# Sample forgetting attention and sample memory attention run beside the two passes of the first projection

## What is computed

```python
# layer 0; h = rmsnorm(x); z = h @ fox_w_in  (q | k | v 1024 each, f 8, xq 512, gate 1536)
lf = log_sigmoid(f + b_f)
mix_p = fox_prompt(q, k, v, lf)                       # causal, decay by cumsum(lf)
k_past = cache_fox_k[page_table]; v_past = cache_fox_v[page_table]; lf_past = cache_fox_logf[page_table]
suf = flip(cumsum(flip(lf_past))) - lf_past           # sum of the gates behind each past key
s_past = q_s @ k_past * scale + suf + c_new           # samples: 8 heads x 4 queries x 2048 past keys
s_new = q_s @ k_new * scale + (c_new_q - c_new_k), causal
p = softmax(concat(s_past, s_new)); mix_s = p @ concat(v_past, v_new)
x = x + rmsnorm((concat(mix, mem_attend(xq, mk, mv)) * silu(gate)) @ w_out)
```

## Time and profile before

| | |
|---|---|
| median of 3 runs | 4196.71 us |
| the profiled execution | 4198.52 us |
| its span, first to last instruction | 4196.9 us |
| TensorE matmul busy | 3607.0 us (86%) |
| VectorE, ScalarE, POOL busy | 1889.5, 1344.0, 338.3 us |
| mean granted TensorE clock | 0.915 of full speed |
| p00 and p01 | 156 to 628 and 684 to 1245 us |
| prompt attention, sample attention | 1302 to 2084, 2084 to 2660 us |

### The profile page before, as it was taken

The page is one execution under the profiler, slowest core; times in us unless marked ns, Lnnn a source line. Parts: engine busy times, 40 slices in busy tenths (PEclk is TensorE's granted clock), DMA queues, the critical chain, the costliest instruction groups (busy, mean ns, idle before and its releaser), DMA issues. The chain is left out here.

```text
span 4196.9 us, 58583 instructions
## 1 busy us (share of the span) xinstructions
PE 3607.0 (86%) x19825; PEld 3129.9 (75%) x19825; DVE 1889.5 (45%) x3376; ACT 1344.0 (32%) x2451; POOL 338.3 (8%) x550
## 2 busy tenths in 40 slices
PE   5699996999986888888678888699599779996899
PEld 4699995888875777777667777488499768775687
DVE  3311114334214766666567878533311244574433
ACT  1211114433113555545345656211211243311111
POOL 0131000000000111101111111000000000131000
PEclk8799997999997999999888989699799889997899
DMA  4332224333323222222176777333222233475332
GB/s 141 98 90 88 92 81 139 123 96 113 121 71 98 82 82 97 107 87 95 32 280 238 269 246 258 112 110 113 73 92 94 94 123 113 144 225 159 125 106 77
DMA packets 385188, 523.10 MB, mean 125 GB/s; under 512 B 52799, under 2 KB 275008, under 8 KB 380423
## 3 DMA queue, kind: packets, MB, share of 16 engines
q1 hardware_dynamic: 317175, 398.59, 29.6%
q0 software_dynamic: 30624, 93.22, 6.4%
q10 hardware_dynamic: 37248, 29.37, 2.2%
HBM read 388.77 MB, written 132.68 MB: 124 GB/s over the span
## 5 line engine op out<-in xcount | busy, mean ns | idle before, releaser
L399 ACT ACTIVATE z_st_p<-bank 128x352 f32<-128x352 f32 (+1 forms) x320 | 165.5, 518 | 933.8 <-PE bank L372 933.5
L345 DVE CAST w_hi_p<-w_raw_p 128x1024 fp32r<-128x1024 f32 (+1 forms) x130 | 89.6, 689 | 772.9 <-PE bank L372 755.6
L1410 PE MATMUL bank<-w_hi_o,b_hi_o 128*128 128x512 f32 x816 | 328.3, 402 | 64.5 <-DVE w_lo_o L1452 64.4
L372 PE MATMUL bank<-h00hi,w_hi_p 128*128 128x352 f32 x984 | 318.2, 323 | 7.0 <-DVE w_lo_p L347 7.0
L1411 PE MATMUL bank<-w_hi_o,b_lo_o 128*128 128x512 f32 x816 | 324.2, 397 | 0.0
L1412 PE MATMUL bank<-w_lo_o,b_hi_o 128*128 128x512 f32 x816 | 324.0, 397 | 0.0
L372 PE MATMUL bank<-h00lo,w_hi_p 128*128 128x352 f32 x984 | 316.0, 321 | 0.0
L372 PE MATMUL bank<-h00hi,w_lo_p 128*128 128x352 f32 x984 | 315.7, 321 | 0.0
L372 PE MATMUL bank<-h01hi,w_hi_p 128*128 128x512 f32 x656 | 264.3, 403 | 9.2 <-DVE w_lo_p L347 7.9
L372 PE MATMUL bank<-h01hi,w_lo_p 128*128 128x512 f32 x656 | 256.3, 391 | 0.0
L372 PE MATMUL bank<-h01lo,w_hi_p 128*128 128x512 f32 x656 | 256.2, 391 | 0.0
(11 more groups left out here) (349 smaller groups left out, 8925.7 us busy)
## 6 DMA issues: line engine op xcount, KB each, us to landing
z<-z_st_p SPq DMA_DIRECT2D x128, 512.0 KB, 2.7
v_raw_sf<-in_cache_fox_v POOLq DMA_DIRECT2D x128, 512.0 KB, 4.9
k_raw_sf<-in_cache_fox_k SPq DMA_DIRECT2D x128, 512.0 KB, 5.0
w_raw_p<-in_fox_w_in SPq DMA_DIRECT2D x80, 512.0 KB, 4.0
b_raw_o<-bT SPq DMA_DIRECT2D x32, 768.0 KB, 7.4
w_raw_p<-in_pool_w_in SPq DMA_DIRECT2D x48, 512.0 KB, 4.7
out<-tok_fa ACTq DMA_DIRECT2D x64, 256.0 KB, 2.3
w_raw_o<-in_w_out ACTq DMA_DIRECT2D x24, 512.0 KB, 3.5
```

What stands on the lines that cost most here:

```text
L372: last = nc.tensor.matmul(out, wt[:, u, k, :], h[:, k, at0:at0 + width], start=(m == 0), stop=(m == MM - 1))
L399: nc.scalar.activation(z_st[:, t % 2, at0:at0 + width], src[:, 0:width], func).then_inc(z_read, 1)
L1410: nc.tensor.matmul(out, bh, w_hi[:, k, cols], start=(k == 0), stop=False)
```

## The change

Three things are moved. The samples' half of the gates, the suffix sums and the new keys and values become a work, `sample_gates`, in tiles 0 to 2 of p01. Sample attention becomes a work, `sample_fox`, in tiles 2 to 32 of p01: page s is transposed in step s, scored in the even step at or behind it with its neighbour, and the value page of step s is that of 19 steps before; it has one bank for scores instead of two, rings of 4 key and 3 value pages, and goes page by page over all samples without a loop. Memory attention of the samples goes from p01 to p00, tiles 18 to 39; that of the prompt to tiles 32 to 41 of p01. What stays of the gates, `prompt_gates`, is a block between p01 and prompt attention; it loads the forget rows from z, where the passes now store them. The comments in the diff are mine.

```diff
 def project_pass(..., stores, works=None, past_gates=None):        # forget=(bias_f, fT) is gone
-                width = FH if row is None else P
-                if row is not None:
-                    sp.wait_ge(z_read, C * (t + 1))
+                _, row, _, width = tiles[t]        # the forget tile is stored to z like any other, 8 rows
+                sp.wait_ge(z_read, C * (t + 1))
...
-def forget_gates(...)      # prompt and samples, a block of its own
+def prompt_gates(nc, const, banks, zT, f_row, bias_f, lf_prompt, cT):      # a block of its own
+            sp.dma_start(fT[:, :], zT[f_row:f_row + FH, 0:SEQ]).then_inc(f_in, 16)
...
-def sample_kv_out(...)     # a block of its own
+def sample_gates(...):     # a Work of 14 steps: sample gates, suffix sums, new keys and values
+            if i == STEPS - 1:
+                sp.wait_ge(row_d, 4)
+                for q in range(TN):
+                    sp.dma_start(sufT.rearrange("(r q) n -> q r n", q=TN)[q], suf_row[:, :]).then_inc(out_d, 16)
+                sp.wait_ge(out_d, 16 * (5 + TN))
...
-def sample_attention(...)  # a block of its own
+def sample_fox(...):       # a Work of STEPS = 3 + 128 + 22 = 153 steps
+    T_BANKS, S_BANK, O_BANKS, M_BANK = banks[0:2], banks[2], banks[3:5], banks[5]
+    def sp(sp):            # step i, s = i - 3
+            if i == 1:
+                for h in range(FH):        # 3 small loads per head: mask, c_key, c_qry
...
+            for x in (range(KR) if i == 0 else [s + KR - 1] if s >= 1 and s + KR - 1 < NPG else []):
+                sp.dma_start(k_raw[:, x % KR, :], cache_k[...]).then_inc(k_in[x % KR], 16)
+    def pe(pe):
+            if group(s) is not None:       # even s: scores of pages s - 2 and s - 1
+                pe.wait_ge(ktl_d, 2 * s)
+                for h in range(FH):
+                    nc.tensor.matmul(S_BANK[:, 0:2 * P], q, kT_hi[:, h, :], ...)
+                    nc.tensor.matmul(S_BANK[:, 0:2 * P], q, kT_lo[:, h, :], ...)
+            for b, p in products(s):       # value tile of page s - 19
+                pe.wait_ge(vl_d, y + 1)
+                for n in range(2):
+                    nc.tensor.matmul(O_BANKS[n][:, :], pr, v_hi[:, y % 2, vs], ...)
+                    nc.tensor.matmul(O_BANKS[n][:, :], pr, v_lo[:, y % 2, vs], ...)
+            if batch(s, 18) is not None:   # transposes of p into M_BANK
+                pe.wait_ge(pn_d, b + 1)
...
+            if 0 <= s < NPG:
+                if s:
+                    pe.wait_ge(ktl_d, 2 * s)
+                for n in range(2):         # 8 transposes of page s
+                        nc.tensor.transpose(T_BANKS[n][...], k_raw[:, s % KR, ...], ident[:, :])
+    def act(act):          # order in a step: kT_hi x2, low rows of the group, exp, pT, v_hi of step s + 1
+    def dve(dve):
+            if i == 2:
+                dve.wait_ge(kn_in, 16 * (1 + 3 * FH))
...
+            if 0 <= s < NPG:               # kT_lo, two halves, each behind its kT_hi
+                nc.vector.tensor_tensor(kT_lo[at], T_BANKS[n][...], kT_hi[at].bitcast(F32), ALU.subtract)
+            if group(s) is not None:
+                nc.vector.scalar_tensor_tensor(dst, dst, c_qry[:, b:b + 1], S_BANK[0:R, 0:2 * P], ALU.add, ALU.add)
+                nc.vector.tensor_tensor(dst, dst, low[0:R, :], ALU.add)
+                if g == NG - 1:            # new keys' scores, then the maximum over 2052 columns
+            if batch(s, 17) is not None:   # wait for exp, reciprocal, multiply 2052 columns
+            for b, p in products(s + 1):
+                dve.wait_ge(vh_d, y + 1)
+                nc.vector.tensor_tensor(v_lo[:, y % 2, :], v_raw[:, y % VR, :], v_hi[:, y % 2, :].bitcast(F32), ALU.subtract)
...
 # first pass (p00)
+                    sample, _ = sample_memory(0, ..., [(XQ + 2, 0), (len(tiles) - 2, 14)], lambda sp: landed(sp, XQ - 1))
 # second pass (p01)
-                        sample, ends = sample_memory(0, ..., [(0, 0), (8, 14)])
-                    prompt, _ = prompt_memory(0, ..., [(8, 0), (XQ + 1, 15), (30, 42)], ...)
+                        gates, ends_g = sample_gates(..., [(0, 0), (2, 14)])
+                        fox, ends_f = sample_fox(..., [(2, 0), (32, 153)], ends_g)
+                    prompt, _ = prompt_memory(0, ..., [(32, 0), (41, 42)], lambda sp: landed(sp, XQ - 1), ends_f)
-            forget_gates(...)
-        sample_kv_out(...)
+        prompt_gates(nc, const, banks, z0, F_ROW, fox_b_f, fox_lf_p, cT)
         fox_attention(nc, const, banks, z0, cT, bT, fox_k_p, fox_v_p)
-        sample_attention(...)
         output_projection(nc, "o0", ...)
```

## The result

The changed kernel takes 4256.8 us (median; 4249.6 to 4259.1) against 4196.8 (4194.2 to 4204.2): ratio 1.0137, 95% interval 1.0119 to 1.0155. Its profiled execution took 4249.6 us, its span is 4248.1: 51.2 more than the span before.

A forecast was written before the change was run, and what follows sets the result against it. In the second pass TensorE is busy 558 of 561 us, so added work costs at least its own TensorE time. -576.6 - 25 + 0 + 12 + 12 + 405 + 183 + 25 = +35: 4234 us, range 4105 to 4310.

The forecast's parts named there:

- The signs named beforehand: In the second pass, odd steps' value matmuls wait over 100 us for the value difference; pass takes 1110 to 1170 us.
- The old stage, -576.6, and the gates, -25: Removed between stages: the sample attention stage, 576.6 us, and 25 us of the 57.4 between second pass and prompt attention.
- Sample memory attention, 0: Moved from second pass to first, where it pays the same 40 us as before: zero in sum.
- Gates in tiles 0 to 2 and prompt memory attention, +12 each: Second pass: gates and new keys/values cost 12 us of TensorE (5 to 22); denser prompt memory attention +12 (0 to 25).
- The page steps, 405 + 183 + 25 = 613: Sample attention in the second pass: 405 us of TensorE's own time, 183 of waits, 25 of lost clock.
- Own TensorE work, 405: In sample attention 128 pages take TensorE 358 us and the further work per sample 47, together 405 us.
- Waits, 183: Waits in sample attention: 115 us between steps, 38 sample ends, 10 first steps and last sample, 20 start; bounds 0, 260.
- The clock, 25: Half rate after some waits of about 2.6 us or longer in sample attention costs 25 us, bounds 0 and 90.
- Cover of the weight splits, 0: In sample attention's steps the weight splits fit into VectorE's idle time and cost nothing; without that cover 57 us.
- Rival 1: Waits in page steps mostly hidden, VectorE's value tile being ready for the odd step: 4112 us, chance 0.27.
- Rival 2: The clock falls in most pairs of page steps, costing 90 us instead of 25: 4297 us, chance 0.13.
- Rival 3: Loads don't keep up at the start and sample ends of sample attention, costing 15 us: 4247 us, chance 0.05.

The follow-up runs named there:

- experiment 6: Kernel before the change, with sample memory attention alone moved from the second pass to tiles 18 to 39 of the first: 4202.4 us against 4199.4, ratio 1.0006.
- experiment 8: Changed kernel with the page steps of sample attention left out of the pass, result columns filled with gate rows: 3620.5 us.
- 1, values first: Changed kernel with ScalarE's copy and VectorE's difference of the next value tile ahead of the work on the key transposes: 4115.2 us, ratio 0.9807.
- 2, longer in even steps: Changed kernel with the difference of the value tile computed twice at the end of even steps 20 to 126: 4347.0 us.
- 7, denser: Changed kernel with the 153 steps of sample attention in 24 tiles instead of 30, prompt memory attention in 15 instead of 9: 4287.5 us.
- 9, best: Changed kernel with value work ahead of key work only in even steps, the start of sample attention taken apart, queries laid out early: 4101.1 us, ratio 0.9763.
- 10, filled: Changed kernel with 6 extra unused matmuls ahead of the wait for the value difference in 41 odd steps: 4224.1 us, ratio 1.0060.
- 11, dense and values first: Changed kernel with value work ahead of key work and the 153 steps of sample attention in 24 tiles instead of 30: 4150.1 us.

## Why the prediction was right, and by which steps

The forecast was +35 us and the range 4105 to 4310; it is +60 by the medians, +51 by the profiles. The sign and the mechanism were right; that the number came so near is in part luck, as the page steps show. The signs named beforehand held: the value matmuls waited 107.7 us for the value difference, and the pass took 1165.6 us to the end of its last matmul. Step by step:

- **The old stage, -576.6, and the gates, -25.** The new block's load to prompt attention's first takes 29.3 us, and 33.5 from the pass's last matmul (1891.6); forecast 32.
- **Sample memory attention, 0.** First pass +42.6 for 40, second -37.0 in experiment 6: at most 5 us off.
- **Gates in tiles 0 to 2 and prompt memory attention, +12 each.** 545 forecast for the pass without page steps, 544 measured. Each alone was not measured.
- **The page steps, 405 + 183 + 25 = 613.** Measured 621 (experiment 8 against the changed kernel), but the three terms were not so good each. The table takes the cost of the page steps apart, in us of the profiled executions: the pass from first matmul to the gates block's load less the 548.4 of experiment 8 (for the kernel before, its stage); TensorE's idle time in the page steps; what half rate costs, which is half of the time that the granted clock was at 1.2 GHz and TensorE not idle; and the rest, own work with drains.

| kernel | page steps | idle | half rate | rest |
|---|---|---|---|---|
| before | 577 | 101 | 54 | 421 |
| changed | 621 | 138 | 54 | 430 |
| 1, values first | 491 | 55 | 17 | 419 |
| 2, longer in even steps | 719 | 201 | 91 | 428 |
| 7, denser | 660 | 169 | 71 | 420 |
| 9, best | 468 | 38 | 11 | 419 |
| 10, filled | 589 | 111 | 18 | 460, 30 of it the added matmuls |
| 11, dense and values first | 517 | 78 | 28 | 411 |

- *Own TensorE work, 405, was too small*: 419 to 421, in the kernel before as in 1 and 9. A pair of page steps is as forecast: on the timeline of kernel 1 one score group starts at 1099.06 and the next at 1108.73, with 18 projection matmuls between, so 9.67 - 18 x 0.227 = 5.6. The excess is therefore at the sample ends; I did not break it down. Some 10 us more in the changed kernel go with its 63 waits for the value difference, as drains.
- *Waits, 183, were too large*: 138. Outside the longest at the sample ends there are 23 of about 0.8 us, 8 of about 1.5 and 21 of 2.13, where I had worked out 1.27 and 2.64. The chain is a little shorter (+3.77 for +4.0), and two slots with the switches cover 2.98 us (1118.19 to 1121.17, the end of the last L365) where I took 2.73. At the sample ends six waits of 3.3 us and five of 2.3 to 3.0 make 34, forecast 38. The start is 21.6 for 20.
- *The clock, 25, was too small*: 54. The step that failed: I took only waits of 2.5 us and more to bring half rate, since a 0.66 us wait had none and the 2.53 us one had the earlier trace rows. Pauses of 2.13 us do it too, as the rows at 1270.83 show, in 16 of 21 cases. Making the waits shorter or removing them took 36 us of half rate away (kernel 10) and 37 (kernel 1), making them longer added 37 (kernel 2).
- **Cover of the weight splits, 0**: they stand behind the value difference in the rows above, as forecast.
- **Rival 1** (waits hidden, 4112) needed a chain under 2.7 us; it was 3.77. The chain can be cut by reordering, though, and then the time is 4115: the rival's price was right for a kernel that was not the one proposed. **Rival 2** (half rate in most pairs, 4297) was half right: in the steady steps it comes after one slot and not after two. The Trainium skill ("TensorE: Matmul & The Clock Gate", A second HAM failure mode: psum-queue depth-cycling) tells of another kernel, whose short and frequent pauses between groups of matmuls made the clock swing. These traces agree with that better than I allowed: 0.93 with the pauses, 0.98 with work in them. In the page steps waits of 0.8 and 1.5 us did no harm and those of 2.13 did. **Rival 3** did not show: beyond the first page TensorE waited for no page load, and kernel 9 moved 221 GB/s in its densest stretch.

The misses in the page steps nearly cancel: 14 more own work, 10 of drains that had no term, 45 less waiting, 29 more clock, 8 us in sum. That they cancel is luck; the sum was closer than its terms.

The first two lines of the table also say why the change is slower. What it took out, 577 us, held 101 us of idle time and 54 of half rate; the same work put into the pass has 138 and 54, and some 10 of drains with them, so the merge lost where it was to gain. Kernel 9 has 38 and 11, and 109 us less than the old stage.

## What to carry to other kernels

Work put beside a stage whose engine has no holes is paid in full, and every hole of the added work that the stage's own work doesn't fill is paid as well, because one queue holds both; so compare the two stages' totals first and expect no gain by overlap alone. Before giving up such a merge, follow the chain from one step's last instruction to the next step's first on the helper engine, and put what the next step needs first ahead of what it needs last: here that order was worth 142 us, where the merge itself cost 60. Which order is right can differ between kinds of step.

## What the runs showed of the hardware that was not expected

Adding 246 matmuls whose result nobody uses made the kernel 33 us faster, by raising the granted clock in that stretch from 0.93 to 0.98. Half rate also came without a longer pause just ahead of it. In kernel 1 the score group at 1168.1 (starts 0.21 us apart instead of 0.12) came 15.6 us after a wait of 2.62, with waits of 0.24 and 0.37 alone in between, and directly after 16 small matmuls of 64 rows that pick a sample's result. In the changed kernel and kernels 1 and 10 seven stretches of half rate begin 1.9 to 3.1 us after the first matmul of such a group, with no wait above 0.4 us in the 6 us before; most of the groups have none behind them. In the kernel before it is every one of the eight: half rate begins 0.9 to 2.6 us after the group's first matmul, ahead of which TensorE waited 1.15 us. This is one of them, and the totals around its start:

```profile
2356.01 2.39 PE L1731 MATMUL bank<-eye_sf,o_sb_sf 64*128 64x32 f32 x16 [1.15 <-ACT o_sb_sf L1777]
```

```profile
2343.70:2357.40 13.70, 11.46 (x79) 1.00 0.66 212
2357.40:2374.40 17.00, 14.27 (x70) 0.50 0.58 193
```

So most of the old stage's 54 us of half rate come at the samples' ends, 14 to 17 us long each time, while its page steps with their shorter waits run at full clock between. Whether the small matmuls or the waits about them bring the clock down was not tried and stays open.
